# The first mixer's step on TensorE: weighing and key products ahead of the scores

## The reference

```
for g, (win, dil) in enumerate(DILATED_GROUPS):      # (128, 1), (512, 4), (2048, 16)
    o, lse = dilated_band_attention(q[:, :, g], k[:, :, g], v[:, :, g], win, dil)
...
s = einsum('nbqhd,nbphd->nhbqp', qb, kk) * SCALE     # scores
probs, lse = masked_softmax_lse(s, mask)
o = einsum('nhbqp,nbphd->nbqhd', probs, vv)          # weighed values
...
y = merge_by_denominator(outs, lses) @ w_o
```

## Time and profile before

| | us |
|---|---|
| median of 3 runs | 3144.2 (3140.66 to 3145.14) |
| profiled execution, its own time | 3148.7 |
| its span, first to last instruction | 3147.1 |
| TensorE busy in the span | 3066.4 (97%) |
| VectorE, ScalarE, GpSimd busy | 1544.0, 1509.2, 1529.8 |
| first mixer: first scores to last scores | 51 to 1114 |
| mean granted clock of TensorE | 0.987 of 2.4 GHz |

### The profile page before, as it was taken

The page is one execution under the profiler, slowest core; times in us unless marked ns, Lnnn a source line. Parts: engine busy times, 40 slices in busy tenths (PEclk is TensorE's granted clock), DMA queues, the critical chain, the costliest instruction groups (busy, mean ns, idle before and its releaser), DMA issues. The chain is left out here.

```text
span 3147.1 us, 55383 instructions
## 1 busy us (share of the span) xinstructions
PE 3066.4 (97%) x21261; PEld 2950.9 (94%) x21261; DVE 1544.0 (49%) x3370; ACT 1509.2 (48%) x3199; POOL 1529.8 (49%) x1313
## 2 busy tenths in 40 slices
PE   8999999999999989999999999999899999999997
PEld 8999999999999959999999999989799999999997
DVE  3233344343433456654563365388666545433543
ACT  4554545555455534444453354367554444533542
POOL 4343444434444415664564475454256645554663
PEclk9999999999999989999999999999999999999998
DMA  6776776777668364444444444321344444544543
GB/s 235 284 252 226 252 258 234 266 258 269 230 240 293 111 212 153 132 139 132 139 134 138 140 138 148 112 64 49 103 156 134 134 138 133 157 135 141 166 144 96
DMA packets 134214, 540.83 MB, mean 172 GB/s; under 512 B 24336, under 2 KB 48544, under 8 KB 131120
## 3 DMA queue, kind: packets, MB, share of 16 engines
q1 hardware_dynamic: 133440, 536.51, 50.6%
q10 hardware_dynamic: 288, 0.52, 0.0%
q0 software_dynamic: 224, 0.26, 0.0%
HBM read 497.55 MB, written 216.85 MB: 227 GB/s over the span
## 5 line engine op out<-in xcount | busy, mean ns | idle before, releaser
L1387 ACT CAST w_hi<-raw 128x1024 fp32r<-128x1024 f32 (+1 forms) x459 | 471.6, 1028 | 860.6 <-PE bank L103 807.6
L101 PE MATMUL bank<-x_hi,w_hi 128*128 128x352 f32 (+1 forms) x2208 | 712.9, 323 | 7.3 <-POOL w_lo L1505 6.0
L102 PE MATMUL bank<-x_lo,w_hi 128*128 128x352 f32 (+1 forms) x2208 | 707.3, 320 | 0.0
L103 PE MATMUL bank<-x_hi,w_lo 128*128 128x352 f32 (+1 forms) x2208 | 703.9, 319 | 0.0
L1505 POOL TENSOR_TENSOR w_lo<-raw,w_hi 128x1024 fp32r<-128x1024 f32 (+1 forms) x230 | 545.7, 2373 | 266.6 <-ACT w_hi L1387 266.6
L1586 DVE TENSOR_TENSOR w_lo<-raw,w_hi 128x1024 fp32r<-128x1024 f32 (+1 forms) x229 | 316.0, 1380 | 727.6 <-ACT w_hi L1387 727.5
L101 PE MATMUL a_gemm<-x_hi,a_w_hi 128*128 128x352 f32 (+1 forms) x1728 | 561.1, 325 | 11.1 <-DVE x_lo L677 11.0
L102 PE MATMUL a_gemm<-x_lo,a_w_hi 128*128 128x352 f32 (+1 forms) x1728 | 553.9, 321 | 0.0
L103 PE MATMUL a_gemm<-x_hi,a_w_lo 128*128 128x352 f32 (+1 forms) x1728 | 551.8, 319 | 0.0
L101 PE MATMUL bank<-t_h_hi,w_hi 128*128 128x352 f32 (+1 forms) x1440 | 463.2, 322 | 3.7 <-DVE t_h_lo L1592 2.3
L103 PE MATMUL bank<-t_h_hi,w_lo 128*128 128x352 f32 (+1 forms) x1440 | 461.8, 321 | 0.0
(11 more groups left out here) (268 smaller groups left out, 4843.5 us busy)
## 6 DMA issues: line engine op xcount, KB each, us to landing
raw<-w_up SPq DMA_DIRECT2D x264, 512.0 KB, 3.7
roll<-cache SPq DMA_DIRECT2D x128, 1023.5 KB
raw<-w_down SPq DMA_DIRECT2D x96, 512.0 KB, 3.5
a_raw<-w_a SPq DMA_DIRECT2D x72, 512.0 KB, 3.9
roll<-cache SPq DMA_DIRECT2D x16, 2044.0 KB
raw<-w_o SPq DMA_DIRECT2D x48, 512.0 KB, 3.7
raw<-w_down SPq DMA_DIRECT2D x48, 384.0 KB, 3.5
vT<-a_vt SPq DMA_DIRECT2D x24, 516.0 KB, 6.3
```

The costliest lines, as they stand in the source:

```text
L101: pe.matmul(out, w_hi, x_hi, start=first, stop=False)
L102: pe.matmul(out, w_hi, x_lo, start=False, stop=False)
L103: return pe.matmul(out, w_lo, x_hi, start=False, stop=last)
L1387: act.copy(w_hi[:, b % RING, cols], raw[:, b % RING, cols]).then_inc(s_whi, 1)
```

## The change

In TensorE's `body` the call of `scores` moves from the first place to the place behind `weigh_values` and `key_products`. In step 97, where there are no scores any more, nothing changes.

```
             def body(u, i, s):
-                if attends(u):
-                    scores(u)
                 if u == NU + 1:
                     spread_stats(0)
                 if attends(u - 2):
                     weigh_values(u - 2)
                 if attends(u) and s == key_step(i):
                     key_products(i)
+                if attends(u):
+                    scores(u)
                 if u == NU - 3:
                     own_products()
```

## The result

The changed kernel took 3155.5 us (median of five, 3154.6 to 3156.7), against 3144.2 in the same comparison: a ratio of 1.0039, interval 1.0029 to 1.005. It is slower by 11.3 us where 6.8 were forecast; the time lies in the range. The profiled execution took 3154.7 (span 3153.1).

What follows compares the result with a forecast made beforehand. TensorE's own instructions bound steps 0 to 91, the loop over VectorE and ScalarE back to TensorE steps 92 to 97. 0 + 1.0 + 5.8 = 6.8 us on 3144.2 gave 3151.0, range 3146 to 3157.

Steps and rivals of the forecast that it cites:

- (a): TensorE's switches of array shape: the new order costs 0 over 92 steps, with 4.1 us possible either way.
- rival 1: In each step the weighing's weights load while the last product runs: 1.5 us of gain, 3142.7; chance 0.07.
- (b): Scores start up to 1.59 us later, moving VectorE's and ScalarE's work behind them; costs about 1.0 us.
- The last pair: Its second spreading of factors has no room: masking moves by 1.03, so TensorE waits about 1.0 us.
- The factors' room: Factors are ready 2.81 us before TensorE takes them; less 1.59 leaves 1.2, hidden six times of seven.
- rival 3: Factors come late, TensorE waits in six or seven pairs, say 0.8 us each: about 3158; chance 0.12.
- In the third pair it was a late weight transfer ... and that does not move: A late weight transfer ended the third pair's factor chain, and the change does not move it.
- (c): The tail, from step 92: weighing and scores wait on VectorE and ScalarE, at a lowered clock; 5.8 us.
- The loop: In the tail, TensorE over VectorE and ScalarE back to TensorE is later by 3.8 us at full clock.
- two slow pairs: Behind the tail's idle times two of three pairs of scores and weighing run slowly: 5.8 for 3.8 us.
- a fuller slow stretch lets the clock rise again: In the tail, a slow stretch is itself fuller, so the clock recovers; a reason for taking two slow pairs.

Runs made afterwards that it cites:

- e6: Against the changed kernel, key products put back behind the scores, weighing still ahead; 3150.0 us, ratio to before 1.0016.
- e5: Against the changed kernel, weighing put back behind the scores, key products still ahead; 3145.6 us, ratio to before 1.0006.
- e2: Against the kernel before, the new order in steps 0 to 91 only, the old order in the tail; 3147.2 us, ratio 1.0011.
- e7: Against the changed kernel, matmuls that nobody reads added in TensorE's waits in the tail; 3151.3 us, ratio to before 1.0026.
- e4: The kernel before run once more with no edit; 3144.8 us, ratio 1.0010.
- e3: The changed kernel run once more with no edit; 3157.7 us, ratio to before 1.0043.
- e10: Against the kernel before, VectorE's turning put ahead of the key addition in one step of four; 3142.8 us, ratio 0.9995.
- e8: Against the changed kernel, VectorE's turning put ahead of the key addition in one step of four; 3148.2 us, ratio to before 1.0011.

## Why the prediction was right, and where it was short

- **(a) The switches, 0: right.** 409.58 us before and after; the pauses are those foretold. This ends rival 1: no load went ahead of its block. The Trainium skill (TensorEngine Tiling (Array Packing), "Tiling Modes") has a change of mode drain the engine, and the trace agrees: 0.17 to 0.33 us at each.
- **(b) The last pair, 1.0: right**, 0.9 to 1.0 (from 7.97 or 8.01 to 8.93 us). The factors' room fell from 2.82 to 1.43, where 1.2 was worked out; rival 3 did not come.
- **(b) What else hangs on VectorE's masks: missed.** The prediction moved "everything that VectorE and ScalarE do behind the scores" by up to 1.59 us and then followed only the factors. The turning stands there too, and its store to memory is on TensorE's path in pair 1, some 20 us later. Over the profiles with the turning in its old place the wait is 1.59 to 2.27 us in the old order and 2.48 to 3.65 in the new: 1.3 us more in the mean, and 1.4 by the store's start. Behind it the granted clock fell in every profile of the new order with the turning in its old place and in e6, as it did once in the old order (before, first profile, wait 2.27); it did not in e5, with a wait of 2.34. In the changed kernel, by stretch:

```profile
268.00:270.00 2.00, 1.24 (x15) 0.89 (x15) 1.86 (x4) 0.85 (x3) 0.93 (x1) 1.00 0.26 108
270.00:272.00 2.00, 2.00 (x13) 1.35 (x12) 0.95 (x5) 1.40 (x4) 0.54 (x1) 0.51 0.05 20
272.00:274.00 2.00, 2.00 (x11) 2.00 (x10) 1.97 (x9) 2.00 (x9) 2.00 (x2) 0.63 0.00 0
```

  Where the clock stays up pair 1 takes 10.55 us and its wait; the slow stretch adds 1.2 to 1.5 to that, 2.2 in e2. Together this is the step that failed: the cover of what hangs on the masks was worked out for the factors alone, and the turning's store, which had none in pair 1, was put at nothing. It cost 2.4 us in the mean of the same profiles.
- **"In the third pair it was a late weight transfer ... and that does not move": half right.** The transfer is where the chain begins, and with the turning ahead it lands earlier and the wait is gone, in both orders, for a reason that stays open. That the change itself lengthens this wait is not shown: 0.56 to 1.31 in the old order, 0.74 to 1.90 in the new, 0.52 and 2.23 in the halves. Behind e5's 2.23 the clock fell too, and the second spreading came 9.3 us behind the first instead of 7.7.
- **(c) The loop, 3.8 at the full clock: right**, 3.55 in e7, of which the keys are 0.57. Counted from the weighing of step 92, the prediction has the next weighing at 5.3, its scores at 6.1, the third weighing at 9.8, the tile 7 spreading at 14.0 and the last scores at 15.0 us; e7 has 5.3, 6.1, 9.8, 13.8 and 14.7. At the low clock of the changed kernel the same points lie at 5.3, 6.1, 10.3, 15.3 and 16.9, and its waits are 2.0, 0.6 and 1.3 where 2.0, 1.5 and 2.1 were foretold: slow instructions fill them.
- **(c) The clock, two slow pairs for 2.0: too small.** It was three blocks of scores, two of weighing and what stands between them (transposes 1.11 for 0.66, spreading 0.69 for 0.42): 2.7 us, or 5.2 in the other profile, where the slow stretch ran on to the last weighing. The argument that a fuller slow stretch lets the clock rise again failed: TensorE was busy for 2.00 of 2.00 us at 1110 to 1112 and stayed slow. The samples' value products start at 1131.19 us for 1123.02 before, 8.2 later where some 7 were foretold.

The sum of the table for the changed kernel against e4 is 2.6 + 0.6 + 0.9 + 6.3 = 10.4 us, and 2.4 + 0.5 + 0.9 + 8.8 = 12.6 in e3; measured were 11.3 and, e3 against e4, 12.9. Against before's first profile, whose clock fell in pair 1 as well, the table gives 8.9, while the two executions differ by 6.0; behind the tail the changed kernel's took 2.2 less, ahead of pair 1 1.1. So the sign, the places that were named and the loop held, and what was missing lay in pair 1 (about 2.4 us) and in the clock of the tail (0.7 to 3.2).

That the time still fell into the range is in part luck: its upper end, 3157, stood there for a loss in (a) and for rival 3, and neither came. The second median of the same kernel, e3's 3157.7, lies beyond it.

## What to carry to other kernels

When a block is pushed back on one engine, follow every instruction that stands behind its results on the other queues, transfers too, up to the next reader of their buffers, however much later. A short wait in front of a stage without slack can cost twice, once itself and once in the clock behind it (in front of pairs 1 and 3 the waits of 2.23 to 3.65 us did in all cases but one, those of up to 1.95 in none); so count all the work that runs until the clock is seen to rise. Where two engines arrive together, as VectorE and GpSimd do in e4, there is no room in making one later and, as e10 shows in pair 1, little gain in making one earlier.

## What the runs showed that was not expected

- A stretch of 409.58 us in which TensorE does not wait is the same to a nanosecond in twelve profiles of ten different kernels.
- VectorE's multiplication of the turning, 128x352 from and to SBUF, takes 0.52 us alone (250.37 in the changed kernel), 0.92 in e8 and 1.59 in e10, where GpSimd's splitting or multiplication runs beside it. Pair 1 lost nothing by that, since VectorE would have waited there for the output copy anyway. In pair 3 of e8 it took 2.53 beside the splitting, and the key addition started 3.84 us behind the split of the landed block where it was 3.15 before.
